# Two heads to a transpose: how the queries of a sparse attention layer are turned and doubled over the partitions

## The reference, cut to what matters

```python
q = apply_rope(rms_norm(q.reshape(B_, S_, NSA_HEADS, dh), q_norm_w), pos)
...
s_c = jnp.einsum('bgqrd,bcgd->bgqrc', qb, k_c) * scale       # compressed keys
s_s = jnp.einsum('bgqrd,bgqnld->bgqrnl', qb, k_g) * scale    # selected blocks
s_w = jnp.einsum('bgqrd,bkgd->bgqrk', qb, k_wb) * scale      # sliding window
```

## Time and profile before

| | |
|---|---|
| Median of 3 runs | 744.64 us (743.92 to 744.94) |
| Span of the profiled execution, first to last instruction | 741.6 us |
| TensorE busy in it | 693.9 us (94%) |
| VectorE busy | 461.9 us (62%) |
| ScalarE busy | 372.8 us (50%) |
| GpSimd busy | 197.8 us (27%) |
| Mean granted clock of TensorE | 0.993 |

### The profile page before, as it was taken

The page is one execution under the profiler, slowest core; times in us unless marked ns, Lnnn a source line. Parts: engine busy times, 40 slices in busy tenths (PEclk is TensorE's granted clock), DMA queues, the critical chain, the costliest instruction groups (busy, mean ns, idle before and its releaser), DMA issues.

```text
span 741.6 us, 10966 instructions
## 1 busy us (share of the span) xinstructions
PE 693.9 (94%) x3951; PEld 584.7 (79%) x3951; DVE 461.9 (62%) x955; ACT 372.8 (50%) x905; POOL 197.8 (27%) x220
## 2 busy tenths in 40 slices
PE   1899999889999999999998999899899999999997
PEld 1888899788788788878876788778677878787775
DVE  3777454645234654568666776677778667776742
ACT  4652535432234435435554565645677555555541
POOL 2112555420223222233121131201376021212120
PEclk9999999999999999999998999999999999999999
DMA  6521131300111111111000111000142010110101
GB/s 214 171 86 29 29 102 35 99 1 29 44 42 44 30 33 39 30 43 30 29 17 13 30 30 28 15 30 30 35 136 86 30 56 31 43 44 29 57 29 57
DMA packets 19206, 36.75 MB, mean 50 GB/s; under 512 B 2641, under 2 KB 3537, under 8 KB 19153
## 3 DMA queue, kind: packets, MB, share of 16 engines
q1 hardware_dynamic: 19152, 36.06, 15.5%
HBM read 31.85 MB, written 4.19 MB: 49 GB/s over the span
## 4 chain that ended last, share of the span: by engine, by line
PE 76%; DVE 11%; ACT 5%; issue 4%; POOL 2%; DMA 2%; SPq 0%; ACTq 0%; DVEq 0%; POOLq 0%
PE pf L1218 9%; PE pf L1219 9%; PE pf L1220 8%; PE tp L1454 7%; PE po L1434 5%; PE pj L1218 5%; PE pj L1219 5%; PE pj L1220 5%; PE sc L1309 4%; PE po L1435 4%; PE sc L1308 4%; PE sc L1218 3%; PE sc L1220 3%; PE sc L1219 3%; DMA qp<-in_wpack 1%
## 5 line engine op out<-in xcount | busy, mean ns | idle before, releaser
L835 ACT CAST pth<-tp 128x512 fp32r<-128x512 f32 (+1 forms) x148 | 86.7, 586 | 139.8 <-PE tp L1454 139.7
L1158 DVE TENSOR_TENSOR ptl<-tp,pth 128x512 fp32r<-128x512 f32 (+1 forms) x148 | 101.9, 689 | 51.4 <-ACT pth L835 48.6
L592 POOL TENSOR_SCALAR qp<-qp,precip,gate 128x64 f32<-128x64 f32 x64 | 38.3, 598 | 213.4 <-DVE precip L1132 213.4
L1454 PE MATMUL tp<-cst,qp 128*128 128x128 f32 (+1 forms) x592 | 90.0, 275 | 3.2 <-issue 2.5
L550 POOL TENSOR_TENSOR fl<-fraw,fh 128x512 fp32r<-128x512 f32 x36 | 47.6, 1322 | 130.6 <-ACT fh L700 130.6
L1218 PE MATMUL pf<-hh,fh 128*128 128x512 f32 x200 | 81.3, 406 | 0.7 <-DVE ub L1101 0.7
L1218 PE MATMUL pj<-wh,hh 128*128 128x256 f32 (+1 forms) x256 | 75.4, 295 | 6.7 <-POOL wl L533 5.4
L1219 PE MATMUL pf<-hl,fh 128*128 128x512 f32 x200 | 78.9, 395 | 0.0
L1220 PE MATMUL pf<-hh,fl 128*128 128x512 f32 x200 | 78.7, 393 | 0.0
L1146 DVE TENSOR_REDUCE nmax<-sc 128x1 f32<-128x128 f32 (+7 forms) x64 | 48.4, 756 | 45.0 <-PE sc L1330 44.6
L1454 PEld LDWEIGHTS tp<-cst,qp 128*128 128x128 f32 (+1 forms) x592 | 66.7, 139 | 9.7 <-issue 3.7
(11 more groups left out here) (192 smaller groups left out, 1642.5 us busy)
## 6 DMA issues: line engine op xcount, KB each, us to landing
fraw<-in_wside SPq DMA_DIRECT2D x36, 256.0 KB, 2.7
qp<-in_wpack SPq DMA_DIRECT2D x28, 256.0 KB, 3.2
qp<-in_x SPq DMA_DIRECT2D x8, 512.0 KB, 3.3
wor<-in_wout SPq DMA_DIRECT2D x16, 256.0 KB, 2.9
xo<-in_x SPq DMA_DIRECT2D x16, 256.0 KB, 2.6
out<-xo SPq DMA_DIRECT2D x16, 256.0 KB, 2.0
qp<-in_wpack SPq DMA_DIRECT2D x5, 224.0 KB, 2.6
mixc<-in_normw SPq DMA_DIRECT2D x1, 512.0 KB, 6.6
```

The costliest lines, as they stand in the source:

```text
L835: nc.scalar.copy(pth[ptn % 2][0:r, :], tp[tpn % 2][0:r, :]).then_inc(pth_ready, 1)
L1158: V.tensor_tensor(ptl[ptn % 2][0:r, :], tp[tpn % 2][0:r, :], pth[ptn % 2][0:r, :].bitcast(F32), ALU.subtract).then_inc(tp_read, 1)
L1454: ins = nc.tensor.transpose(tp[tpn % 2][0:r, h * P:(h + 1) * P], src, ident)
```

## The change

The copies of the queries by GpSimd and the tile `qd` go. TensorE turns the rows of `qn` themselves, two heads to a transpose: 128 columns are heads 2m and 2m+1, so the first head comes out in partitions 0 to 63 and the second in 64 to 127, 256 columns in all. ScalarE and VectorE now do the doubling: each writes `qh` or `ql` with four instructions of 64 partitions, one for each pair of source half a and destination half r.

```diff
-                qd = sb("qd", [P, GH, 2, HD], F32, d)
...
+        def head_pairs(q, a):
+
+            return q[:, :, :].rearrange("p (m a) q -> p a m q", a=2)[:, a]
...
-            def copy_queries(u):
-
-                i, g = UNITS[u]
-                if u >= 1:
-                    pool.wait_ge(qh_ready, u)
-                src = qn[:, i, g * 256:(g + 1) * 256].rearrange("p (h d) -> p h d", h=GH)
-                for twice in range(2):
-                    ins = nc.gpsimd.tensor_copy(qd[:, :, twice, :], src)
-                ins.then_inc(qd_ready, 1)
...
-            entry_through(pool, NE - 1)
-            pool.wait_ge(q_normed, 2)
-            copy_queries(0)
...
-                if u:
-                    copy_queries(u)
...
             def queries(u):            # ScalarE
...
-                nc.scalar.copy(qh[:, :, :], tp[tpn % 2][:, :].rearrange("p (h q) -> p h q", h=GH)).then_inc(qh_ready, 1)
+                pairs = tp[tpn % 2][:, 0:2 * P].rearrange("p (m q) -> p m q", m=2)
+                for a in range(2):
+                    for r in (0, HD):
+                        ins = nc.scalar.copy(head_pairs(qh, a)[r:r + HD], pairs[a * HD:(a + 1) * HD])
+                ins.then_inc(qh_ready, 1)
...
             def queries(u):            # VectorE
...
-                V.tensor_tensor(ql[:, :, :], tp[tpn % 2][:, :].rearrange("p (h q) -> p h q", h=GH),
-                                qh[:, :, :].bitcast(F32), ALU.subtract).then_inc(tp_read, 1)
+                pairs = tp[tpn % 2][:, 0:2 * P].rearrange("p (m q) -> p m q", m=2)
+                for a in range(2):
+                    for r in (0, HD):
+                        ins = V.tensor_tensor(head_pairs(ql, a)[r:r + HD], pairs[a * HD:(a + 1) * HD],
+                                              head_pairs(qh, a)[r:r + HD].bitcast(F32), ALU.subtract)
+                ins.then_inc(tp_read, 1)
...
             def queries(u):            # TensorE
...
-                pe.wait_ge(qd_ready, u + 1)
+                i, g = UNITS[u]
+                if u == 0:
+                    pe.wait_ge(q_normed, 2)
                 if tpn >= 2:
                     pe.wait_ge(tp_read, tpn - 1)
-                for h in range(GH):
-                    ins = nc.tensor.transpose(tp[tpn % 2][:, h * P:(h + 1) * P],
-                                              qd[:, h, :, :].rearrange("p u d -> p (u d)"), ident)
+                for m in range(2):
+                    ins = nc.tensor.transpose(tp[tpn % 2][:, m * P:(m + 1) * P], tiles(qn[:, i, :], 2 * g + m), ident)
                 ins.then_inc(tp_done, 1)
```

More of the change, by code:

```diff
@@ L355, in hybrid_layer @@
         woh_ready, wol_ready = sem("woh_ready"), sem("wol_ready")
-        qd_ready, qh_ready, kend_ready = sem("qd_ready"), sem("qh_ready"), sem("kend_ready")
+        qh_ready, kend_ready = sem("qh_ready"), sem("kend_ready")
         s_done, max_ready, exp_done = sem("s_done"), sem("max_ready"), sem("exp_done")
```

## The result

The changed kernel takes 767.67 us in the median of 4 runs (766.5 to 775.7), the kernel before 744.71. The ratio is 1.033, 95% interval 1.029 to 1.038, that is 769.5 us by the ratio: slower, as forecast, but by 23 to 25 us and not by 17.7. The median lies just under the upper end of the range, the ratio's value above it. Three of the four runs lie at 766.5 to 768.1 us with a mean granted clock of 0.987 to 0.989, the fourth at 775.7 with 0.976: it is this one that lifts the ratio's value. The profiled execution took 767.26 us with a span of 765.4.

What follows compares the result with a forecast made beforehand. TensorE, busy for 94% of the span, was taken as the bound. Losses of 21.3 us less savings of 2.9 and 0.7 gave +17.7: span 741.6 to 759.3, plus 3.1 for runs, 762 us; range 752 to 768, chance 0.8.

Steps and rivals of the forecast that it cites:

- GpSimd and TensorE: Unit 0's wait for GpSimd's copies goes, -0.7 us; two transposes fewer save 0.22 us in 13 units, -2.9 us.
- The price of the half-height instructions: Four pieces end to end at qh and ql: ScalarE 1.53 us, VectorE 1.72 us, ql 1.97 us later.
- The lower price with overlap: Rival: the new instructions overlap, ql only 1.34 us later, net +8.7, 753.4 us; chance 0.27, including part made up.
- That TensorE loses this less the room: Behind ql, TensorE loses the 1.97 us lateness less the room at the tightest place, read unit by unit.
- The sum, +17.7: Whole kernel: 21.3 us lost on TensorE less 2.9 and 0.7 saved; chance 0.52 for 758 to 766 us.
- the sum of the losses, 21.3: TensorE's losses over five groups of units: 5.9 + 7.0 + 4.4 + 2.1 + 1.9 us.
- a rival with 0.12: Clock falls after TensorE's longer waits, 3.4 us each: one more gives 766 us, two 769; chance 0.12 for over 766.
- Units 6, 9, 11, 12: Room of 0.15 to 0.37 us, flush waiting for ptl in unit 9; together they lose 7.0 us.
- 5, 7, 8, 10: Units with 0.60 to 0.89 us of room, part of ScalarE's lateness hidden in 5 and 8; lose 4.4 us.
- Units 13 to 15: The flush behind the second turn already waits for ptl, so no room: 3 x 1.97 = 5.9 us lost.
- ScalarE's queue: Exponentials behind qh, 0.94 us late, have more room at every score but units 6, 9, 11, 12, where flush loses more.
- The rival "faster": Four half-height instructions take hardly longer than one: 4.2 us kept, 740.4 us; break-even 0.55 us of lengthening; chance 0.05.

Runs made afterwards that it cites:

- the run with the gain alone: Changed kernel with the doubling left out, ScalarE and VectorE each using one full-height instruction (heads mixed, layer not computed): 738.91 us, ratio 0.993.
- ScalarE's or VectorE's half alone: Kernel before, four transposes and GpSimd's copies kept, only ScalarE's cast or only VectorE's subtraction in four half-height instructions: 752.61 us or 757.21 us.
- the same work with a way 0.76 us shorter: Changed kernel with ScalarE signalling twice a unit, so VectorE works on the first source half while ScalarE copies the second: 757.57 us, ratio 1.020.
- the run with both splits: Kernel before with ScalarE's cast and VectorE's subtraction each in four half-height instructions, four transposes and GpSimd's copies kept: 775.83 us, ratio 1.042.
- when VectorE was freed: Changed kernel with two ScalarE signals a unit and VectorE's queries part after the next step's maxima, before the convolution in units 2 and 4: 748.97 us.
- ScalarE's new order: ScalarE's exponentials ahead of its query copies, added to the changed kernel with two signals and VectorE's queries part after the next maxima: 749.16 us, ratio 1.006.

## Why the prediction was right and wrong

**GpSimd and TensorE.** Right. -2.9 and -0.7 us were forecast, the run with the gain alone has -3.9 from the first query on, and dropping two transposes saves 0.22 us a unit in the changed kernel too.

**The price of the half-height instructions.** Right: ScalarE's four take 1.50 us (1.53 forecast), VectorE's 1.73 (1.72), `ql` comes 1.95 us later behind the transposes (1.97). The lower price with overlap did not come. The rule of the Trainium skill by which a VectorE instruction is held when an operand's start quadrant changes (VectorE: DVE Perf Modes, Two Vector instructions with no wait between them) would hold each of the three that follow: the trace agrees, 1.73 us for four of 0.42.

**That TensorE loses this less the room.** Right as a mechanism: ScalarE's or VectorE's half alone cost 8.3 and 12.7 us, both 23.9 with five falls of the clock taken off at 1.6 us each, more than their sum; the same work with a way 0.76 us shorter costs 10 to 12 us less. That the added busy time as such is what costs is excluded by the last of these.

**The sum, +17.7.** Too small. In the trace the loss is 22.3, 4.6 more, and the step that failed is the sum of the losses, 21.3: it put the clock at nothing, and it read the room of eight units too large. The terms:
- Clock: unit 4 lost 1.6 us more through a fall behind its wait of 2.07 us. I had held a fall for a rival with 0.12 and priced it at 3.4 us. It is common: five in the run with both splits, four that the kernel before has not in the repetition of the changed kernel. But one of 3.41 us counts for 1.6, and the long one of 6.83 that the prediction priced for 2.2. In unit 11 the clock fell as well, but the unit lost 2.16 us here and 2.10 in the run with both splits, where it did not fall: the wait for GpSimd's `wol`, 1.31 us before and 1.39 in that run, was 0.47 here and took the fall up. The clock is also what carries the ratio's value, 769.5, over the end of the range at 768: the run of 775.7 us is the one with the lowest clock, and the other three are at 766.5, 767.3 and 768.1.
- Units 6, 9, 11, 12 (7.0 forecast, 8.3 measured) and 5, 7, 8, 10 (4.4, 5.6), 2.5 us together, counting the 0.22 as saved apart (unit 11: not at all). I had looked for the tightest place among scores, turns and `flush` alone. In unit 6 there is a tighter one, the first matmul of a side tile that waits until VectorE has read the last tile of its bank. Before, it was a wait of 0.22 us, so there was no room:

```profile
373.54 0.50 PE L1218 MATMUL pf<-hh,fh 128*128 128x512 f32 x1 [0.22 <-DVE ub L1101]
```

It is 0.46 us after (382.43). Unit 9 has one like it, of 0.45 us before and 0.59 after, unit 12 one (for VectorE's `xo`) of 0.11 and 0.68. The excess of units 11 and 5, 7, 8 and 10 was not traced to one place.
- Units 13 to 15: 5.9 forecast, 6.4 measured, 0.15 each. Behind one subtraction over all partitions VectorE's next instruction starts before its end (the maxima at 599.75, `ql` ending at 599.83); behind the last of the four it starts 0.03 us after it. So what follows `ql` is 0.1 us later still.

**Not in the sum.** 1.5 us of the difference of the spans is the start, ahead of all edits; it differs between runs.

**ScalarE's queue.** The prediction said that it has more room at every score than the 0.94 us, but in four units. It did not look at `pth`, the cast behind the exponentials. In units 13 to 15 ScalarE's end of `pth` (600.66) and VectorE's end of the maxima (600.70) were equally tight in the kernel before:

```profile
599.88 0.82 DVE L1151 TENSOR_REDUCE nmax<-sc 128x1 f32<-128x640 f32 x1
...
600.07 0.59 ACT L835 CAST pth<-tp 128x512 fp32r<-128x512 f32 x1
```

So VectorE's lateness hid ScalarE's in the trace after. It came out with ScalarE's split alone, 1.0 us in each of these units, and when VectorE was freed.

**The rival "faster".** It asked for a lengthening under 0.55 us, and the lengthening is 1.95. The run with the gain alone shows what it would have brought: 738.9 us, where 740.4 was worked out.

**Open.** What makes the clock fall behind one wait and not behind an equal one. Whether ScalarE's new order is worth anything in the changed kernel. Where units 5, 7, 8 and 10 lose the 1.2 us beyond the forecast.

## What to carry to other kernels

Half the partitions at half the columns is not a quarter of the work for ScalarE or VectorE: here four such pieces took two and a half times as long as the one instruction, on the way of a value that everything behind it in the same queue had to wait for. When TensorE is the bound, 0.22 us of its time is cheap to save only if the other engines' lateness stays under the room; and the room is to be read at every semaphore that TensorE takes for the next few microseconds, at banks coming free as well. Where engines hand over in order, first put what is already ready ahead of what must wait: that alone, without touching the way the queries are made, left the kernel 0.5 to 0.7% faster, whereas the 3.9 us that the change saves were lost several times over.

## What the runs showed of the hardware that was not expected

- The granted clock fell to 0.50, the lower level of 1.2 GHz, for 3.41 or 6.83 us at a time, in the attention steps always beside one or two waits of TensorE, of 0.7 to 2.6 us each. Waits of the same length in the same kernel had a fall in one run and none in another: the 2.07 us of unit 4 of the changed kernel with, and the same wait in its repetition without, where the stretch behind it has a granted clock of 1.00:

```profile
324.39 0.44 PE L1305 MATMUL sc<-kst,qh 128*128 128x384 f32 x1 [2.07 <-DVE ql L1009]
...
324.90:328.30 3.40, 3.40 (x20) 2.90 (x19) 2.75 (x8) 1.34 (x5) 1.07 (x2) 1.00 0.00 0
```

  In the two stretches of 3.40 us TensorE has 20 matmul records at 1.00 and 11 at 0.50. A fall of 3.41 us cost 1.6 us, one of 6.83 us 2.2.
- Consecutive copies of ScalarE from or to another half of the partitions start 0.38 us apart at 0.37 us each, a pair over all partitions 0.28 us apart: ScalarE does not overlap them, as VectorE does not. It goes with the change of half and not with the height: ScalarE's 64-partition casts of `pth` (L827, 0.58 us), behind which the half stays, are followed after 0.48 us, nine times in the trace after. So the lost overlap makes about 0.1 us for each of the three that follow, 0.3 of ScalarE's 0.9; the rest is that each piece takes 0.37 us by itself.
